# Residual kept in its own order, a step of eight in the gather's weights, and the router's matmuls in another order

## The chip, the cores and the metric

The kernel runs on one core of one Trainium2 chip. The metric is the device time of one execution in microseconds (us). The engines are TensorE (PE, with its weight loads listed as PEld), VectorE (DVE), ScalarE (ACT), GpSimd (POOL) and SyncE (SP), whose queue issues the large transfers.

## The reference, cut to what matters

The reference runs two transformer blocks over 256 tokens of width 1024. The first one ends with a mixture of 32 experts, chosen in two steps (one of 4 groups, then 2 of its 8 experts):

```python
x = x + gt1 * (merged @ w_out)
h2 = rmsnorm(x, norm2_g) * (1.0 + sc2) + sh2
group_logits = h2 @ rg_w + rg_b
exp_logits = (h2 @ re_w + re_b).reshape(-1, 4, 8)
g_sel = argmax(group_logits)
top_v, top_i = top_k(exp_logits of group g_sel, 2)
y = y + (silu(h2 @ w_gate[e]) * (h2 @ w_up[e]) * gate) @ w_down[e]   # for each chosen expert e
x = x + gt2 * y
```

## The kernel before, in words

Everything is fp32. Each large product is made of three matmuls of fp32r operands (high part and low part, lines 532 to 534), whose weights come from DRAM once. The kernel is one program in which each engine walks the same plan of weight pieces; semaphores join them. The five queues of orders are written out by hand, so an engine does its work in the order of the code.

The stretch around the change is this. The output projection `wo` ends in two column halves g of 512 (two token tiles t each). VectorE adds each result to the residual x (lines 2408 and 2411). ScalarE squares x for the norm (line 1635, `x_square`). TensorE transposes each 128 x 512 part of x (`x_turn`, line 795), ScalarE copies it to SBUF (`x_copy`, line 1627, into `rF`), and TensorE multiplies it with the scaled router weights, 36 columns (`router`, line 803). Logits of both token tiles are accumulated over g = 0 and g = 1. `warm(n)` (line 760) issues n matmuls whose results nobody reads; an fp32 matmul of this kind is two records in the trace, a transpose is one. ScalarE walks in the order square (1, 0), copy (1, 0), square (1, 1), copy (1, 1), square root of the sums.

The route is then a chain of some 15 small VectorE instructions (lines 2070 to 2111), after which TensorE forms ranks (`route`, lines 854 to 863), VectorE writes one-hot slot matrices `Sx` in three parts of 2, 3 and 3 sets of slots (`slots_of`, line 2031), and TensorE picks the tokens with them: `gather(g, banks)`, line 775, has x as the weights and `Sx` as the streaming operand. The first gather runs in `route()`, the other two in `experts()`, behind the first set's up and gate products. The gathers take x times the norm factor in two fp32r parts: the high part is written by ScalarE (`x_high`, line 1406), the low part by VectorE (`x_low`, line 2019), into `xs`. The expert products need 8 chunks k of the width; chunk k is made of columns k, k + 8, k + 16 and so on, since the expert weights lie so in DRAM. Before, `x_high` and `x_low` do this reordering while they read:

```python
inc(e.activation(by8(xs[0], i), x[:, i, :].rearrange("p (c k) -> p k c", k=8), ACT.Copy, ...
```

and a gather matmul takes its weights in one piece, `xs[part][:, i, 128 * k:128 * k + 128]`. Each gather has 32 matmuls: 8 chunks k times two parts times two token tiles. In the first one four banks are filled side by side through all four passes, which are ordered (part, tile) = (0, 0), (0, 1), (1, 0), (1, 1); VectorE does `x_low(0)`, `slots_of(0)`, `x_low(1)`, `slots_of(1)` in this order. VectorE (line 2043) and ScalarE (line 1418) evict the results in turn into `XG`.

Expert weights come through a ring of slots of 1 MB, 17 before the first use, 14 of them used again. The SyncE queue refills a slot when TensorE has done its last matmul on it (`("exu", q, s)`, given by `up` at line 888 and `down` at line 899).

Another place uses a step of 8 on the weights' side already: line 616, `acc[g][:, k:512:8]`, 64 columns, plain fp32.

Of the kernel before, what the change touches and what calls it, by code (L numbers as in the profile page):

```python
# [6 lines left out]
F32 = mybir.dt.float32  # L7
# [3 lines left out]
ALU = mybir.AluOpType  # L11
ACT = mybir.ActivationFunctionType
# [112 lines left out]
def rv(ap):  # L125
    return ap.bitcast(F32R)
# [6 lines left out]
def build(nc, a, out, scr):  # L133
    with ExitStack() as ctx:
# [3 lines left out]
        def mem(off, n):  # L138
            placed[0] += 1
            return nc.alloc_sbuf_tensor_at(f"m{placed[0]}", [128, n], F32, offset=base + 4 * off)[:, :]  # L140
# [27 lines left out]
        x = mem(22304, 2048).rearrange("p (t n) -> p t n", t=2)  # L168
# [12 lines left out]
        def K(c, n=128):  # L181
            return KC[:, c:c + n]
# [3 lines left out]
        def tiny(n):  # L186
            o = top[0]
            top[0] += n
            assert top[0] <= 512
            return small[:, o:o + n]  # L190
# [149 lines left out]
        def skey(p, what):  # L340

            return (what, p.j)
# [11 lines left out]
        ss1, ssr, ssf = tiny(2), tiny(2), [tiny(2) for _ in range(9)]  # L354
# [36 lines left out]
        xs = [rv(mem(o, 2048).rearrange("p (t n) -> p t n", t=2)) for o in (26912, 28960)]  # L391
# [34 lines left out]
        for n in range(4):  # L426
            o = 33312 if n == 2 else 29216
# [29 lines left out]

            return min(last_wo + 1 if p.j <= last_wo else len(plan), p.j + NH)

        def by8(z, i):  # L460

            return z[:, i, :].rearrange("p (k c) -> p k c", k=8)

        def heads(head):

            gens, h = [], 0
            while h < 8 or gens:
                if h < 8 and len(gens) < 5:
                    gens.append(head(h))
                    h += 1  # L470
                for g in list(gens):
                    if next(g, "end") == "end":
                        gens.remove(g)
                yield
# [32 lines left out]
        def tensor(e, w):  # L507
# [16 lines left out]
            def full(ins, *key):  # L524
                then_inc(ins, f"full{where_is[key]}", ("full", key))
# [17 lines left out]
            def parts(p, o, n):  # L543
                return rv(p.H)[:, o:o + n], rv(p.L)[:, o:o + n]
# [212 lines left out]
            def warm(n):  # L757

                for _ in range(n):
                    e.matmul(bank[where_is["wo", 0, 1]][:, 0:128], K(C_ID), K(C_ONE), start=True, stop=True)  # L760

            def gather(g, banks):

                q0, q1 = parts_of[g]
                n = 128 * (q1 - q0)
                per = 512 // n
                o = {}
                for ks in ([(0, 2, 4, 6), (1,), (3,), (5,), (7,)] if per > 1 else [(k,) for k in range(8)]):
                    for part, i in ((0, 0), (0, 1), (1, 0), (1, 1)):
                        w.wait_ge("xs", part, i)  # L770
                        w.wait_ge("Sx", g, i)
                        for k in ks:
                            if (part, i) == (0, 0) and k % per == 0:
                                o[k // per] = take(banks[k // per % len(banks)], "ga", g, k // per)
                            ins = e.matmul(o[k // per][:, k % per * n:k % per * n + n], xs[part][:, i, 128 * k:128 * k + 128],  # L775
                                           rv(Sx[:, i, 128 * q0:128 * q1]), start=(part, i) == (0, 0),
                                           stop=(part, i) == (1, 1))
                            if (part, i) == (1, 1) and k % per == per - 1:
                                full(ins, "ga", g, k // per)
# [8 lines left out]
            def x_turn(g, ts=(0, 1)):  # L788

                for t in ts:  # L790
                    w.wait_ge("x1", t, g)
                    b = take("s", "r", g, t)
                    for c in range(4):
                        o = 512 * g + 128 * c
                        ins = e.transpose(b[:, 128 * c:128 * c + 128], x[:, t, o:o + 128], K(C_ID))
                    full(ins, "r", g, t)

            def router(g, b, ts=(0, 1)):
                for t in ts:
                    w.wait_ge("taken", ("r", g, t))  # L800
                    w.wait_ge("rWg")
                    for c in range(4):
                        ins = e.matmul(b[t][:, 0:36], rF[g][:, c, 128 * t:128 * t + 128], rWg[:, 4 * g + c, :],
                                       start=g == 0 and c == 0, stop=g == 1 and c == 3)
                    if g:
                        full(ins, "lg", t)

            def w_out():
                o, lg = {}, {}

                def step(p, t):
                    for i in range(p.m):
                        k = p.k + i
                        w.wait_ge("mgL", k // 2)
                        if k == 0:
                            o[t] = take("m", "wo", p.g, t)
                        rows = slice(128 * t, 128 * t + 128)
                        ins = three(o[t][:, :], (mgT[0][:, k, rows], mgT[1][:, k, rows]), parts(p, 512 * i, 512),
                                    k == 0, k == 7)
                    return ins  # L820
                held = []
                for p in walk("wo"):
                    w.wait_ge(*skey(p, "L"))
                    if p.k < 4:
                        for t in range(2):
                            ins = step(p, t)
                        used(ins, p)
                        continue
                    held.append(p)
                    if p.k < 6:  # L830
                        if p.g:
                            x_turn(0)
                            lg = [take("s", "lg", t) for t in range(2)]
                        continue
                    for t in range(2):
                        for h in held:
                            ins = step(h, t)
                            if t:
                                used(ins, h, *([("wo", p.g, 1)] if h is p else []))
                        if t == 0:  # L840
                            full(ins, "wo", p.g, 0)
                    held.clear()
                    if p.g == 0:
                        continue
                    x_turn(1, (0,))
                    router(0, lg)
                    x_turn(1, (1,))
                    router(1, lg, (0,))
                    warm(3)
                    router(1, lg, (1,))  # L850
                    warm(10)

# [238 lines left out]
            for p in walk("ik"):  # L1091
                w.wait_ge(*skey(p, "L"))
                b = take("m", "ik")
                for k in range(8):
                    ins = three(b[:, 0:256], parts(p, 128 * k, 128), (hT[0][:, k, :], hT[1][:, k, :]), k == 0, k == 7)
                used(ins, p, ("ik",))
            for p in walk("iw"):
                w.wait_ge(*skey(p, "L"))
                for t in range(2):
                    b = take("m", "iw", t)  # L1100
                    rows = slice(128 * t, 128 * t + 128)
                    for k in range(8):
                        ins = three(b[:, 0:8], (hT[0][:, k, rows], hT[1][:, k, rows]), parts(p, 8 * k, 8), k == 0, k == 7)
# [33 lines left out]
            for q in range(2):  # L1137
                b = take("s", "ws", q)
                for g in range(4):
                    ins = e.transpose(b[:, 128 * g:128 * g + 128], wsr[:, 512 * q + 128 * g:512 * q + 128 * g + 128], K(C_ID))  # L1140
# [15 lines left out]
            for p in walk("kk"):  # L1156
                w.wait_ge(*skey(p, "L"))
                b = take("m", "kk2", p.g)
                for k in range(8):
                    w.wait_ge("kv", k // 2)  # L1160
                    ins = three(b[:, 0:256], parts(p, 128 * k, 128), (kvT[0][:, k, :], kvT[1][:, k, :]), k == 0, k == 7)
# [14 lines left out]
        def scalar(e, w):  # L1176
# [3 lines left out]
            def inc(ins, what, *keys):  # L1180
                then_inc(ins, "act_" + what, *keys)
# [220 lines left out]
            def x_high():  # L1402
                w.wait_ge(*skey(G["wo"][-1], "used"))
                for i in range(2):
                    w.wait_ge("rrec")
                    inc(e.activation(by8(xs[0], i), x[:, i, :].rearrange("p (c k) -> p k c", k=8), ACT.Copy,
                                     scale=ssr[:, i:i + 1]), "xs", ("xs", 0, i))

            def gather(g):
                q0, q1 = parts_of[g]  # L1410
# [133 lines left out]
            o = 0  # L1544
# [14 lines left out]
            for cp in range(4):  # L1559
                w.wait_ge("taken", ("h", cp))  # L1560
                o = slice(512 * cp, 512 * cp + 512)
# [141 lines left out]
        def vector(e, w):  # L1703
# [4 lines left out]
            def inc(ins, what, *keys):  # L1708
                then_inc(ins, "dve_" + what, *keys)
# [306 lines left out]

            def x_low(i):
                w.wait_ge("xs", 0, i)
                inc(e.scalar_tensor_tensor(out=by8(xs[1], i), in0=x[:, i, :].rearrange("p (c k) -> p k c", k=8),
                                           scalar=ssr[:, i:i + 1], in1=by8(xs[0], i).bitcast(F32), op0=ALU.mult,  # L2020
                                           op1=ALU.subtract), "xs", ("xs", 1, i))

            def slots_of(g):

# [316 lines left out]
            for cp in range(4):  # L2341
# [3 lines left out]
                o = slice(512 * cp, 512 * cp + 512)  # L2345
# [82 lines left out]
            for i in range(2):  # L2428
                for g in range(8):
# [4 lines left out]
                                                 op1=ALU.mult), "mix", i, g)  # L2434
# [392 lines left out]
```

## Time and profile before

| what | us |
|---|---|
| median of 3 runs (2296.68 to 2307.59) | 2299.89 |
| the profiled execution's own time | 2299.89 |
| its span, first to last instruction | 2297.8 |
| TensorE busy | 2003.5 |
| VectorE busy | 1092.4 |
| ScalarE busy | 857.8 |

Mean granted clock of TensorE: 0.954 of full speed. Durations come from the one profiled execution; its time is 2.1 us over its span. The page says which engines are busy; the chain that ended last says which of this work sets the end; the windows say what DMA and clock did meanwhile; the timeline gives starts and durations of single instructions.

### The profile page before, as it was taken

The numbers are of one execution on the slowest core, as the hardware profiler recorded it, in microseconds if no ns is written. First come the engines' busy times: TensorE is split into PE (matmuls) and PEld (weight loads), VectorE is DVE, ScalarE is ACT, GpSimd is POOL, SyncE is SP. The second block draws the span as 40 slices with busy tenths as digits, with TensorE's granted clock in tenths as the row PEclk, the third lists the DMA queues.
The fourth block names the chain that finished last, engine by engine and source line by source line (L and its number), as shares of the span: only waits on it lengthen the run. The fifth ranks groups of instructions, "written<-read, shape, count | busy, mean of one in ns | idle before, by whom it ended". The sixth has DMA issues, their size and how long they took to land.

```text
span 2297.8 us, 30304 instructions
## 1 busy us (share of the span) xinstructions
PE 2003.5 (87%) x12871; PEld 1627.8 (71%) x12871; DVE 1092.4 (48%) x1359; ACT 857.8 (37%) x1110; POOL 136.9 (6%) x112
## 2 busy tenths in 40 slices
PE   3998899999999767776759998799998999959998
PEld 2998788888997211111139997678998999858997
DVE  5545576557764111111135555654555555485554
ACT  2444335544443100000034444335445444554443
POOL 0013312000210000000000000200000000030000
PEclk9989899999999998889889999899999999999999
DMA  8542343557888999999965554544554555304551
GB/s 309 171 129 92 92 148 129 168 199 238 283 313 329 393 424 423 423 423 424 423 233 188 186 182 156 177 147 148 184 195 134 185 185 184 125 19 156 184 184 72
DMA packets 243935, 503.16 MB, mean 219 GB/s; under 512 B 9562, under 2 KB 163507, under 8 KB 218835
## 3 DMA queue, kind: packets, MB, share of 16 engines
q1 hardware_dynamic: 243136, 500.27, 60.4%
q8 instruction: 104, 1.70, 0.3%
q10 hardware_dynamic: 514, 0.73, 0.1%
q0 software_dynamic: 144, 0.17, 0.1%
q14 instruction: 37, 0.30, 0.0%
HBM read 500.07 MB, written 1.06 MB: 218 GB/s over the span
## 4 chain that ended last, share of the span: by engine, by line
PE 70%; DMA 17%; DVE 6%; ACT 3%; issue 2%; POOL 1%; SPq 0%; DVEq 0%; ACTq 0%; POOLq 0%
PE bank L532 20%; PE bank L534 20%; PE bank L533 20%; DMA m<-in_expert_w_up 7%; DMA m<-in_expert_w_gate 7%; PE bank L888 3%; PE bank L590 2%; DVE m L1735 1%; PE bank L643 1%; ACT m L1244 1%; DMA m<-in_ada_w 1%; DMA m<-in_expert_w_down 1%; DMA m<-in_w_in 1%; PE bank L775 1%; PE bank L899 0%
## 5 line engine op out<-in xcount | busy, mean ns | idle before, releaser
L532 PE MATMUL bank<-m,m 128*128 128x256 f32 (+2 forms) x3240 | 1026.3, 317 | 23.2 <-DVE m L1735 20.0
L533 PE MATMUL bank<-m,m 128*128 128x256 f32 (+2 forms) x3240 | 1012.4, 312 | 0.0
L534 PE MATMUL bank<-m,m 128*128 128x256 f32 (+2 forms) x3240 | 1012.2, 312 | 0.0
L1735 DVE TENSOR_TENSOR m<-m,m 128x1024 fp32r<-128x1024 f32 x508 | 629.2, 1242 | 490.1 <-ACT m L1201 488.8
L1201 ACT ACTIVATE m<-m 128x1024 fp32r<-128x1024 f32 x508 | 534.7, 1058 | 463.1 <-PE bank L534 432.5
L532 PEld LDWEIGHTS bank<-m,m 128*128 128x128 f32 x3240 | 617.9, 191 | 67.1 <-DVE m L1735 22.2
L533 PEld LDWEIGHTS bank<-m,m 128*128 128x128 f32 x3240 | 617.9, 191 | 38.4 <-issue 2.4
L534 PEld LDWEIGHTS bank<-m,m 128*128 128x128 f32 x3240 | 616.8, 190 | 37.1
L888 PE MATMUL bank<-m,m 128*32 128x512 f32 x1024 | 192.5, 690 | 72.8 <-DMA m<-in_expert_w_up 47.6
L888 PEld LDWEIGHTS bank<-m,m 128*32 128x32 f32 x1024 | 42.0, 123 | 213.3 <-DMA m<-in_expert_w_up 86.8
L899 PE MATMUL bank<-m,m 128*32 128x512 f32 x512 | 96.8, 677 | 44.0 <-DMA m<-in_expert_w_down 36.9
L899 PEld LDWEIGHTS bank<-m,m 128*32 128x32 f32 x512 | 21.1, 120 | 113.3 <-DMA m<-in_expert_w_down 70.7
L2165 DVE SCALAR_TENSOR_TENSOR m<-bank,m,m 128x512 f32<-128x512 f32 x8 | 6.0, 750 | 173.3 <-PE bank L888 173.3
L590 PE MATMUL bank<-m,m 128*128 128x128 f32 x256 | 43.2, 348 | 47.3 <-DVE m L1797 41.4
L2171 DVE TENSOR_TENSOR m<-bank,m 128x512 f32<-128x512 f32 x16 | 10.3, 686 | 150.9 <-PE bank L899 150.9
L590 PEld LDWEIGHTS bank<-m,m 128*128 128x128 f32 x256 | 42.1, 262 | 49.8 <-issue 49.8
L1491 ACT ACTIVATE m<-m 128x512 fp32r<-128x512 f32 x44 | 27.8, 632 | 107.7 <-DVE m L2244 107.7
L1749 DVE SCALAR_TENSOR_TENSOR m<-m,m,m 128x512 f32<-128x512 f32 x84 | 63.1, 751 | 8.3 <-DMA m<-in_ada_w 5.5
L1430 ACT ACTIVATE m<-m 128x512 fp32r<-128x512 f32 x16 | 9.3, 630 | 142.3 <-DVE m L2171 142.3
L1447 ACT ACTIVATE m<-bank 128x512 f32<-128x512 f32 x8 | 4.8, 597 | 147.3 <-PE bank L923 147.3
L1485 ACT ACTIVATE m<-bank 128x512 f32<-128x512 f32 x44 | 26.3, 598 | 71.1 <-PE bank L534 71.1
L2562 POOL TENSOR_TENSOR m<-m,m 128x2048 f32<-128x2048 f32 x1 | 6.6, 6601 | 774.0 <-DMA m<-in_a_ln_b 774.0
(312 smaller groups left out, 1286.1 us busy)
## 6 DMA issues: line engine op xcount, KB each, us to landing
m<-in_ffn_w_in SPq DMA_DIRECT2D x88, 1024.0 KB, 5.1
m<-in_w_in SPq DMA_DIRECT2D x66, 1024.0 KB, 5.1
m<-in_expert_w_gate SPq DMA_DIRECT2D x64, 1024.0 KB, 25.5
m<-in_expert_w_up SPq DMA_DIRECT2D x64, 1024.0 KB, 24.2
m<-in_expert_w_down SPq DMA_DIRECT2D x64, 1024.0 KB, 25.6
m<-in_ffn_w_out SPq DMA_DIRECT2D x44, 1024.0 KB, 4.9
m<-in_ada_w SPq DMA_DIRECT2D x24, 1024.0 KB, 5.5
m<-in_a_w_in SPq DMA_DIRECT2D x16, 1024.0 KB, 5.2
```

What stands on the lines that cost most here:

```text
L532: e.matmul(o, s[0], m[0], start=first, stop=False, skip_group_check=skip)
L533: e.matmul(o, s[0], m[1], start=False, stop=False, skip_group_check=skip)
L534: return e.matmul(o, s[1], m[0], start=False, stop=last, skip_group_check=skip)
L590: ins = e.matmul(o, v, D[:, 128 * (i % 2):128 * (i % 2) + 128], start=True, stop=True)
L643: ins = e.matmul(b[:, 128 * g:128 * g + 128], K_[:, c], Q_[:, c2], start=True, stop=True)
L888: ins = e.matmul(b[32 * j:32 * j + 32, :], XG[:, q, k, 32 * j:32 * j + 32], ld.raw[:, 512 * i:512 * i + 512], start=k == 0, stop=k == 7, s ...
L899: ins = e.matmul(b[n][32 * j:32 * j + 32, :], eT[q % 2][:, 128 * c + 32 * j:128 * c + 32 * j + 32], ld.raw[:, 1024 * i + 512 * n:1024 * i ...
L1201: inc(e.activation(rv(fit(q.H, q.view.shape)), q.view, ACT.Copy), "h", skey(q, "H"))
L1485: taken(e.activation(fb[4], b[:, :], ACT.Silu), p.name, p.g, also=[("fs", n, c)])
L1491: inc(e.activation(fb[2 * (c % 2)].rearrange("p c n -> p (c n)"), fb[5], ACT.Copy), "ffn", ("fH", n, c))
L1735: inc(e.tensor_tensor(rv(fit(q.L, q.view.shape)), q.view, fit(q.H, q.view.shape), ALU.subtract), "l", skey(q, "L"))
L1749: ins = e.scalar_tensor_tensor(out=acc[g], in0=p.view[:, k, :], scalar=cs[:, 4 * q + k:4 * q + k + 1], in1=acc[g], op0=ALU.mult, op1=ALU.add)
```

## The change

`x_high` and `x_low` write `xs` in the order of x, and the helper `by8` is gone. The gathers take chunk k as every eighth column of `xs`, with a step of 8 elements (32 bytes) from one weight column to the next. At the end of the output projection, `router(0)` stands ahead of the transposes of (1, 0); the second transposes follow `router(1)` of tile 0; and three groups of `warm` (4, 2 and 4 matmuls) take the place of one of 3. The last `warm(10)` stays.

```diff
--- before.py
+++ after.py
@@ -457,10 +457,6 @@
 
             return min(last_wo + 1 if p.j <= last_wo else len(plan), p.j + NH)
 
-        def by8(z, i):
-
-            return z[:, i, :].rearrange("p (k c) -> p k c", k=8)
-
         def heads(head):
 
             gens, h = [], 0
@@ -772,7 +768,7 @@
                         for k in ks:
                             if (part, i) == (0, 0) and k % per == 0:
                                 o[k // per] = take(banks[k // per % len(banks)], "ga", g, k // per)
-                            ins = e.matmul(o[k // per][:, k % per * n:k % per * n + n], xs[part][:, i, 128 * k:128 * k + 128],
+                            ins = e.matmul(o[k // per][:, k % per * n:k % per * n + n], xs[part][:, i, k:1024:8],
                                            rv(Sx[:, i, 128 * q0:128 * q1]), start=(part, i) == (0, 0),
                                            stop=(part, i) == (1, 1))
                             if (part, i) == (1, 1) and k % per == per - 1:
@@ -842,11 +838,13 @@
                     held.clear()
                     if p.g == 0:
                         continue
+                    router(0, lg)
                     x_turn(1, (0,))
-                    router(0, lg)
+                    warm(4)
+                    router(1, lg, (0,))
+                    warm(2)
                     x_turn(1, (1,))
-                    router(1, lg, (0,))
-                    warm(3)
+                    warm(4)
                     router(1, lg, (1,))
                     warm(10)
 
@@ -1403,8 +1401,7 @@
                 w.wait_ge(*skey(G["wo"][-1], "used"))
                 for i in range(2):
                     w.wait_ge("rrec")
-                    inc(e.activation(by8(xs[0], i), x[:, i, :].rearrange("p (c k) -> p k c", k=8), ACT.Copy,
-                                     scale=ssr[:, i:i + 1]), "xs", ("xs", 0, i))
+                    inc(e.activation(xs[0][:, i, :], x[:, i, :], ACT.Copy, scale=ssr[:, i:i + 1]), "xs", ("xs", 0, i))
 
             def gather(g):
                 q0, q1 = parts_of[g]
@@ -2016,9 +2013,8 @@
 
             def x_low(i):
                 w.wait_ge("xs", 0, i)
-                inc(e.scalar_tensor_tensor(out=by8(xs[1], i), in0=x[:, i, :].rearrange("p (c k) -> p k c", k=8),
-                                           scalar=ssr[:, i:i + 1], in1=by8(xs[0], i).bitcast(F32), op0=ALU.mult,
-                                           op1=ALU.subtract), "xs", ("xs", 1, i))
+                inc(e.scalar_tensor_tensor(out=xs[1][:, i, :], in0=x[:, i, :], scalar=ssr[:, i:i + 1],
+                                           in1=xs[0][:, i, :].bitcast(F32), op0=ALU.mult, op1=ALU.subtract), "xs", ("xs", 1, i))
 
             def slots_of(g):
```

## Rows read from the trace of the kernel before

**Rows 1.** The page, shares of the chain that ended last, by engine.
```profile
PE 70%; DMA 17%; DVE 6%; ACT 3%; issue 2%; POOL 1%; SPq 0%; DVEq 0%; ACTq 0%; POOLq 0%
```

**Rows 2.** The chain in order of time (start us, us, what).
```profile
713.55 2.06 DVE m L2019
...
715.66 2.65 PE bank L775 x20
...
737.61 11.31 PE bank L775 x64
...
765.59 21.18 DMA m<-in_expert_w_up
```

**Rows 3.** Windows: busy us (instructions) by engine, clock, DMA share, GB/s.
```profile
716.00:718.00 2.00, 2.00 (x19) 2.00 (x18) 1.70 (x6) 0.61 (x2) 0.00 (x0) 1.00 0.00 0
...
758.00:759.00 1.00, 1.00 (x16) 0.36 (x12) 0.00 (x0) 0.00 (x0) 0.00 (x0) 1.00 0.00 0
900.00:1000.00 100.00, 70.45 (x343) 16.16 (x337) 9.24 (x14) 4.13 (x7) 0.00 (x0) 0.86 1.01 423
```

**Rows 4.** Vector lines: duration ns min/median/max, first and last start, form.
```profile
L1201 ACT ACTIVATE m<-m x508: 250/1060/1166, 36.1 to 2276.6; 128x1024 fp32r<-128x1024 f32 x170
...
L1406 ACT ACTIVATE m<-m,m x2: 2138/2148/2157, 706.5 to 708.5; 128x1024 fp32r<-128x1024 f32 x2
...
L2222 DVE SCALAR_TENSOR_TENSOR m<-m,m,m x4: 1277/1282/1285, 1180.3 to 2293.3; 128x1024 f32<-128x1024 f32 x4
...
L2019 DVE SCALAR_TENSOR_TENSOR m<-m,m,m x2: 2067/2105/2143, 710.8 to 713.5; 128x1024 fp32r<-128x1024 f32 x2
```

**Rows 5.** Timeline, 703 to 740 us (start us, us, engine, line).
```profile
703.02 1.87 PE L803 MATMUL bank<-m,m 128*128 128x36 f32 x16
...
704.72 0.64 PE L795 MATMUL bank<-m,m 128*128 128x128 f32 x4
...
705.39 0.60 ACT L1627 ACTIVATE m<-bank 128x512 f32<-128x512 f32 x1 [0.44 <-PE bank L795]
...
706.01 0.91 PE L760 MATMUL bank<-m 128*128 128x128 f32 x6
...
706.47 4.20 ACT L1406 ACTIVATE m<-m,m 128x1024 fp32r<-128x1024 f32 x2 [0.29 <-DVE m L2072]
...
706.76 0.98 PE L803 MATMUL bank<-m,m 128*128 128x36 f32 x8
...
710.83 2.07 DVE L2019 SCALAR_TENSOR_TENSOR m<-m,m,m 128x1024 fp32r<-128x1024 f32 x1
...
711.94 0.91 PE L760 MATMUL bank<-m 128*128 128x128 f32 x6
712.80 0.75 DVE L2031 TENSOR_TENSOR m<-m,bank 128x256 fp32r<-128x256 f32 x2
...
713.36 1.67 PE L775 MATMUL bank<-m,m 128*128 128x256 f32 x12 [0.51 <-DVE m L2031]
...
718.24 10.51 PE L888 MATMUL bank<-m,m 128*32 128x512 f32 x96
...
739.24 0.68 ACT L1418 ACTIVATE m<-bank,m 128x384 f32<-128x384 f32 x1 [13.26 <-PE bank L775]
```

**Rows 6.** Weight loads: three lines' durations as in rows 4, a timeline row.
```profile
L1064 PEld LDWEIGHTS bank<-m,m x32: 137/137/137, 2035.6 to 2066.2; 128*64 128x64 f32 x32
...
L775 PEld LDWEIGHTS bank<-m,m x96: 186/188/192, 713.3 to 748.4; 128*128 128x128 f32 x96
...
L616 PEld LDWEIGHTS bank<-m,m x64: 195/218/220, 471.6 to 555.5; 128*64 128x64 f32 x64
...
471.65 2.00 PEld L616 LDWEIGHTS bank<-m,m 128*64 128x64 f32 x16
```

**Rows 7.** Windows, columns as in rows 3.
```profile
708.00:710.00 2.00, 2.00 (x19) 1.86 (x17) 1.79 (x12) 2.00 (x2) 0.00 (x0) 1.00 1.01 422
...
732.40:735.60 3.20, 3.20 (x17) 0.78 (x20) 0.38 (x2) 0.00 (x0) 0.00 (x0) 0.50 1.01 428
```

## The prediction

> **What bounds the kernel now.** I read the page's shares of the chain first, to see which parts of the program can set the end at all. TensorE holds 70% and DMAs 17% [rows 1]. The diff touches one stretch only: the end of the output projection, the router, and the gathering of tokens for the experts, about 702 to 749 us. So the question is whether this stretch is on the chain. The chain in order of time says yes: it goes through VectorE's `x_low(1)` at 713.55, then TensorE's gather matmuls at 715.66 and 737.61, and only at 765.59 does it pass to the DMAs of the expert weights [rows 2].
>
> Next I asked whether the DMA stream absorbs a delay of TensorE, since it fills the experts' time. The windows say no. The stream runs at 423 GB/s through the experts, but it stands at 0 GB/s at 716 to 718 us and again at 758 to 759 us [rows 3]. Both times every slot of the ring is full, and a slot comes free only when TensorE has used it: `up(0, 0)` comes right behind the first gather, `down(0, 4)` behind the second and third. After the second gap the share stays at 1.01, so the end of the experts is the end of that gap plus a fixed number of bytes. A delay of the gathers delays the first restart by the first gather's part and the second restart by the whole. It passes one for one to the end, and so does a gain. Nothing of 700 to 760 us is free on TensorE; VectorE and ScalarE matter only where TensorE waits for them.
>
> **Part 1: contiguous writing of the residual.** In the kernel before, `x_high` and `x_low` read x with a step of 8 elements. They take 2148 and 2105 ns apiece for 1024 elements; the contiguous neighbours of the same width, a ScalarE copy and a VectorE scalar_tensor_tensor, take 1060 and 1282 ns [rows 4]. So the two on ScalarE give up 2 x 1.09 = 2.2 us, and the two on VectorE 2 x 0.82 = 1.6 us. ScalarE's gain counts nothing: its pair started at 706.47 and had ended when VectorE began `x_low(0)` at 710.83 [rows 5], and after it starts at about 708.7 and ends at 710.9, under the route's small VectorE chain, which ends at 712.6 (part 2). Were that cover gone it would be worth up to 2.2 us. VectorE's 0.82 us of `x_low(0)` lies ahead of `slots_of(0)`, for which the first gather waits; that of `x_low(1)` ends the pause in the middle of that gather (below).
>
> **Part 2: the order on TensorE.** I count records. Between the last projection matmul and the end of the last `router(1)`, before has 16 of `router(0)`, 4 transposes, 4 transposes, 8, 6 of `warm(3)` and 8, which is 46. After has the same work with 4 + 2 + 4 warm matmuls in place of 3, which is 14 records more. A warm record takes (706.76 - 706.01)/6 = 0.125 us, a router record (704.72 - 703.02)/16 = 0.106 us [rows 5]. By that 14 x 0.125 = +1.75 us. Does TensorE wait besides? By the same rows `router(0)` starts four transposes before 703.02, at 702.6, and ends at 704.3, the transposes of (1, 0) end at about 704.9, and their copy on ScalarE (0.60 us [rows 5]) at about 705.5, under `warm(4)`, which lasts to 705.75. The transposes of (1, 1) end at 707.7, their copy at 708.3, under `warm(4)` again, to 708.54. So no wait is added, and the last `router` starts at 708.5 where it started at 706.76. VectorE's logits for t = 1 wait for it, and with them the whole route: +1.75 us. On ScalarE the square of (1, 1) now stands behind a later copy, and the square root behind both; it comes at about 708.3, the reciprocal at 708.5, still ahead of the logits at 709.5. Without warm matmuls' cost the move would be nearly neutral.
>
> Together: `x_low(0)` starts at 710.83 + 1.75 = 712.58. `slots_of(0)` started 1.97 us behind it and now does so 1.15 us behind, at 713.73 (the ranks stand ahead of `warm(3)` on TensorE and are there). TensorE started 0.56 us after that, at 713.36; by this it would at 714.29, but its own `warm(3)`, six records from 711.94 [rows 5], leaves it free 1.75 us later than it did, at 711.94 + 0.75 + 1.75 = 714.44. So the first gather starts there, **+1.08 us**. Its pause is gone: the fourth pass needed `x_low(1)`, for which it stood until 715.66 [rows 2]; now that ends at 713.73 + 0.66 + 1.28 = 715.7 and TensorE comes to it after 12 matmuls, not before 716.0.
>
> **Part 3: the gather's weights with a step of 8.** This decides. Each of the 96 gather matmuls loads 128 columns of `xs` as weights, contiguous before and 32 bytes apart after. The trace of before has no strided fp32r load of 128 columns, so I bound it. Contiguous loads take 137 ns for 64 columns and 188 for 128 [rows 6]: a fixed 86 ns and 0.80 ns a column, so that 128 columns hold the loader for some 102 ns. Line 616 has exactly the new step, `acc[g][:, k:512:8]`, with 64 columns: 195 ns at least and 218 at the median, against 137. Less 86 that is 109 to 132 ns for 64 columns, and 16 of them in a row span 2.00 us, so one each (2.00 - 0.22)/15 = 0.119 us [rows 6]. Doubled, these are 0.218 to 0.264 for 128 columns, with 0.238 between. The other engines pay alike for the same step: (2148 - 1060)/1024 = 1.06 ns more an element on ScalarE [rows 4], and the weights (119/64 - 0.80) = 1.06 ns more a column. I take 0.24 us, twice the measured spacing. The ends that I keep are 0.129 (no cost, below) and 0.350 us (86 + 2 x 132, no load overlapping the next one).
>
> The weights can be loaded while the matmul before runs, so a gather matmul takes the longer of load and stream. Before, the first gather's last 20 took (718.24 - 715.66)/20 = 0.129 us [rows 2, 5], and the 64 of the other two, 384 wide, 11.31 us or 0.177 us each [rows 2]. Then:
> - first gather: 32 x 0.24 = 7.68 us in place of 718.24 - 713.36 = 4.88 us, which is +2.80; with the late start **+3.88 us**
> - second and third: 64 x 0.24 = 15.36 in place of 11.31, **+4.05 us**. The evictions, 0.67 us a bank on alternating engines [rows 5], stay under 4 x 0.24 = 0.96, since a bank holds one k and takes four matmuls.
>
> Sum +7.9 us. The profiled execution took 2299.89 us (span 2297.8, the rest lies around it), which is also the median of the three, so the forecast is 2299.9 + 7.9 = **2307.8 us**, +0.34%. With 0.218 it is 1.08 + 2.10 + 2.64 = +5.8 (2305.7), with 0.264 it is 1.08 + 3.57 + 5.59 = +10.2 (2310.1): the forecast's own range, with a little of noise, is 2305 to 2311.
>
> **Rivals.** *The step costs the weight load nothing.* For it: nothing but that line 616 is plain fp32 in two records, and a load of 64 columns. Against it: 218 ns beside 137. Then the first gather is 32 x 0.129 = 4.1 us from 714.44, it ends at 718.55, and all is +0.3 us: 2300.2. 
>
> *The loads don't overlap at all.* One mechanism: each strided load holds the loader for its full 350 ns. Then 32 x 0.350 = 11.2 (+6.3, with the start +7.4) and 64 x 0.350 = 22.4 (+11.1), +18.5 us: 2318.4, slower by 0.8%. Against it: line 616 starts a load every 119 ns while each lasts 218. It decides (over 11.5 us) from 0.277 us a load, where 96 loads cost the missing 3.6 us more.
>
> *The clock falls.* The granted clock went to 0.50, the lower level of 1.2 GHz, at 732.4 to 735.6 us, behind `slot_gates`, whose matmuls stream four columns each [rows 7]. The strided loads thin TensorE's stream of columns as well. If the clock fell through the second and third gather, a matmul of 384 columns would take 384/1.2 = 0.32 us in place of 0.24: 64 x 0.08 = +5.1 more, 2312.9. Against: behind the router's 36-column matmuls the clock is 1.00 at 708 to 710 [rows 7], and behind the pause in the first gather it is 1.00 at 716 to 718 [rows 3].
>
> *Faster.* The step free and the route not late either, because the copies on ScalarE were what ended last. Then the first gather starts at about 712.9 and ends at 717.0, -1.3 us: 2298.6. The records before show no wait of the router for a copy, which speaks against it; and even that is not 0.5%.
>
> **How the numbers follow.** Chances: forecast 0.62, step free 0.15, loads apart 0.09, clock 0.11, faster route 0.03. The range is 2299 to 2314: it takes in the free step and the clock and leaves out most of the loads apart and of the faster route. About 0.5% (11.5 us) is what a measurement can tell from no change. Faster by more than that: 0.03, for noise alone, as no case gives it. Slower: loads apart and the clock case nearly whole, and the upper end of the forecast: 0.27. Same: 0.70.
>
> **What the profile after would show.** Weight loads of the gather line at about 350 ns instead of 188, and matmuls 0.24 us apart in all three gathers; 1.06 us for `x_high` and 1.28 us for `x_low`; the last `router` about 1.75 us later; no pause in the first gather; DMA gaps that end about 3.9 and 7.9 us later. Wrong would be loads of 190 ns (then 2300), spacings over 0.28 us, or a DMA stream that still restarts at 759 us, by which the delay would have been absorbed.

## The result: 0.5% slower, and the profile after

| | us |
|---|---|
| before, median of 9 | 2300.91 |
| changed, median of 9 | 2313.01 |
| ratio | 1.0051, 95% interval 1.0039 to 1.0062 |
| the profiled execution of the changed kernel | 2311.64, span 2309.6 |

The ratio stands for +11.7 us, with an interval of 9.0 to 14.3. A second set of runs of the same kernel (e8 below) gave 1.0043, 1.0027 to 1.0059, which is +9.9 us. The forecast was +7.9 us, 2307.8, with 2305 to 2311 for the forecast case alone; the measured 2313.0 lies outside that and inside the whole range of 2299 to 2314.

The gather line decided the forecast, so it comes first. These are its weight loads and its matmuls in the profile after: duration in ns (min/median/max), then first and last start.

```profile
L771 PEld LDWEIGHTS bank<-m,m x96: 312/338/343, 709.4 to 753.5; 128*128 128x128 f32 x96
L771 PE MATMUL bank<-m,m x96: 352/404/570, 709.4 to 753.7; 128*128 128x384 f32 x64, 128*128 128x256 f32 x32
```

A load takes 338 ns where it took 188 [rows 6]. The timeline after answers to [rows 5]:

```profile
703.51 1.04 PE L799 MATMUL bank<-m,m 128*128 128x36 f32 x8
...
703.90 2.19 ACT L1404 ACTIVATE m<-m,m 128x1024 fp32r<-128x1024 f32 x2 [0.30 <-DVE m L2068]
...
707.63 1.28 DVE L2016 SCALAR_TENSOR_TENSOR m<-m,m,m 128x1024 fp32r<-128x1024 f32 x1
...
708.75 0.91 PE L756 MATMUL bank<-m 128*128 128x128 f32 x6
708.83 0.75 DVE L2027 TENSOR_TENSOR m<-m,bank 128x256 fp32r<-128x256 f32 x2
...
709.42 7.97 PE L771 MATMUL bank<-m,m 128*128 128x256 f32 x32
...
717.32 10.51 PE L886 MATMUL bank<-m,m 128*32 128x512 f32 x96
```

The times of this stretch are nearly all earlier than before, although the kernel is slower: the parts ahead of the diff vary from one execution to the next. So the two can only be laid over each other from a common point. I take VectorE's last product of the output projection (line 2408, in the changed kernel 2404), which is the last start in these rows of before and of the changed kernel:

```profile
L2408 DVE TENSOR_TENSOR m<-bank,m x4: 684/692/692, 691.6 to 702.8; 128x512 f32<-128x512 f32 x4
```
```profile
L2404 DVE TENSOR_TENSOR m<-bank,m x4: 683/690/692, 686.8 to 697.9; 128x512 f32<-128x512 f32 x4
```

Counted from there, the points in the table repeat to 0.1 us between the two executions of before, of the changed kernel and of e6. The table has all kernels of this study, in us from the common point: the start of the first expert matmul (`up(0, 0)`), of the first of `down(0, 4)`, and the landing of the last expert weights, for which TensorE waits on the chain.

| kernel | common point (us from the start) | `up(0, 0)` | `down(0, 4)` | last weights |
|---|---|---|---|---|
| before | 702.8 | +15.4 | +51.9 | +461.5 |
| before again (e11) | 699.4 | +15.5 | +51.9 | +461.5 |
| changed | 697.9 | +19.4 | +61.9 | +472.7 |
| changed again (e8) | 699.4 | +19.4 | +61.9 | +472.6 |
| e1 order only | 700.3 | +17.2 | +55.3 | +464.9 |
| e2 step only | 700.9 | +17.7 | +56.9 | +468.3 |
| e3 neither | 699.6 | +13.8 | +48.6 | +458.2 |
| e4 steps 1 to 8 | 699.9 | +16.3 | +55.2 | +465.0 |
| e5 delay | 697.8 | +24.8 | +61.3 | +470.8 |
| e6 `down` first | 701.9 | +15.4 | +37.2 | +457.4 |
| e12 the same again | 699.1 | +15.5 | +37.3 | +457.3 |
| e7 `down` first, changed kernel | 699.9 | +19.4 | +41.2 | +463.9 |
| e9 as e6, no inner warm | 701.1 | +14.9 | +36.7 | +456.7 |
| e10 order without warm | 698.2 | +20.0 | +54.8 | +465.3 |

So the changed kernel has its last expert weights 11.2 us later. The chain after (start us, us, what), to be read beside [rows 2], says where most of them come from:

```profile
709.66 7.72 PE bank L771 x32
717.39 10.44 PE bank L886 x96
727.82 4.39 PE bank L868 x32
732.21 6.14 PE bank L886 x32
738.36 15.74 PE bank L771 x64
```

The first gather has no pause and 0.241 us a matmul; the other two take 15.74 us where they took 11.31. In between, `slot_gates` and `up(0, 3)` take 10.53 us. The same two rows of before are

```profile
728.74 3.71 PE bank L870 x32
732.45 5.16 PE bank L888 x32
```

that is 8.87 us, with the same instructions. The windows of the changed kernel tell why (busy us by engine, clock, DMA share, GB/s; to be read beside [rows 3, 7]):

```profile
710.00:712.00 2.00, 2.00 (x10) 2.00 (x9) 1.79 (x4) 0.00 (x0) 0.00 (x0) 0.52 0.03 12
712.00:714.00 2.00, 2.00 (x10) 2.00 (x10) 0.00 (x0) 0.00 (x0) 0.00 (x0) 0.63 0.00 0
714.00:716.00 2.00, 2.00 (x10) 2.00 (x10) 0.99 (x2) 0.49 (x2) 0.00 (x0) 1.00 0.00 0
732.00:736.00 4.00, 4.00 (x21) 1.11 (x25) 0.38 (x2) 0.00 (x0) 0.00 (x0) 0.50 1.01 426
...
762.00:764.00 2.00, 2.00 (x24) 0.77 (x20) 0.00 (x0) 0.00 (x0) 0.00 (x0) 1.00 0.03 8
764.00:766.00 2.00, 2.00 (x24) 0.79 (x20) 0.00 (x0) 0.00 (x0) 0.00 (x0) 1.00 0.73 168
```

The lower clock lasts longer between the gathers than it did. It is also there in the first gather, where ten matmuls pass in 2 us at 0.52, at 0.63 and at 1.00 alike. That gather goes at the pace of its weight loads, and the clock costs it nothing: it took 7.72 us here, and 7.70 in e7 below, where the same gather ran wholly at 1.00. The second stop of the DMA stream ends after 764 us, which is +66 from the common point; before it ended after 759, which is +56 [rows 3].

### The profile page after: what moved, and what is told of

It reads as the page before. It is cut to its first block, busy times and chain, and to the rows that moved or that the text cites. A ratio compares the mean times of both kernels' runs of the same rounds, so it can differ in the third digit from the quotient of the medians.

```text
span 2309.6 us, 30332 instructions
## 1 busy us (share of the span) xinstructions
PE 2021.6 (88%) x12885; PEld 1638.4 (71%) x12885; DVE 1089.7 (47%) x1359; ACT 855.4 (37%) x1110; POOL 136.6 (6%) x112
## 4 chain that ended last, share of the span: by engine, by line
PE 71%; DMA 16%; DVE 6%; ACT 3%; issue 2%; POOL 1%; SPq 0%; ACTq 0%; DVEq 0%; POOLq 0%
PE bank L528 20%; PE bank L530 20%; PE bank L529 20%; DMA m<-in_expert_w_up 7%; DMA m<-in_expert_w_gate 6%; PE bank L886 3%; PE bank L586 2%; DVE m L1732 1%; PE bank L771 1%; PE bank L639 1%; ACT m L1242 1%; DMA m<-in_expert_w_down 1%; DMA m<-in_w_in 1%; PE bank L897 1%; DMA m<-in_ada_w 0%
## 5 line engine op out<-in xcount | busy, mean ns | idle before, releaser
L530 PEld LDWEIGHTS bank<-m,m 128*128 128x128 f32 x3240 | 615.9, 190 | 37.2
L886 PE MATMUL bank<-m,m 128*32 128x512 f32 x1024 | 198.1, 715 | 73.0 <-DMA m<-in_expert_w_up 46.6
L897 PE MATMUL bank<-m,m 128*32 128x512 f32 x512 | 99.9, 697 | 39.4 <-DMA m<-in_expert_w_down 32.2
L586 PEld LDWEIGHTS bank<-m,m 128*128 128x128 f32 x256 | 41.7, 260 | 48.6 <-issue 48.6
```

Of the source, the lines that this page charges most:

```text
L530: return e.matmul(o, s[1], m[0], start=False, stop=last, skip_group_check=skip)
L586: ins = e.matmul(o, v, D[:, 128 * (i % 2):128 * (i % 2) + 128], start=True, stop=True)
L886: ins = e.matmul(b[32 * j:32 * j + 32, :], XG[:, q, k, 32 * j:32 * j + 32], ld.raw[:, 512 * i:512 * i + 512], start=k == 0, stop=k == 7, s ...
L897: ins = e.matmul(b[n][32 * j:32 * j + 32, :], eT[q % 2][:, 128 * c + 32 * j:128 * c + 32 * j + 32], ld.raw[:, 1024 * i + 512 * n:1024 * i ...
```

## The experiments

**The parts of the diff, one at a time.** The first one keeps the old gather and the old writing and takes the new order:

```diff
-                    x_turn(1, (0,))
                     router(0, lg)
-                    x_turn(1, (1,))
+                    x_turn(1, (0,))
+                    warm(4)
                     router(1, lg, (0,))
-                    warm(3)
+                    warm(2)
+                    x_turn(1, (1,))
+                    warm(4)
                     router(1, lg, (1,))
```

> The kernel before with TensorE's new order at the end of the output projection and nothing else: x is still read with the step, the gather's weights are contiguous. Measured from the end of the output projection. Theory (14 more warm records push the whole route): last router 1.7 us later, first gather starts 1.7 us later, its pause stays, and all ends +1.7 us, 2302.6 where before has 2300.9. Rival (the order is what costs, by the clock or by a wait for a copy on ScalarE): +5 us or more, and a stall ahead of a router in the trace.

Measured: 1.0025, 1.0013 to 1.0036, +5.8 us. In the trace the route came 1.7 us later, `up(0, 0)` 1.8 us, and there was no stall. Another 1.7 us came behind it, again between the gathers:

```profile
714.86 2.66 PE bank L775 x20
...
727.96 4.67 PE bank L872 x32
732.63 5.86 PE bank L890 x32
738.49 11.34 PE bank L775 x64
```

4.67 + 5.86 = 10.53 us as in the changed kernel, and the last weights come 3.4 us later. The theory of the 14 records holds for its part, 1.7 us. As a forecast of the whole time, +1.7 us, it failed: the interval, 3.0 to 8.3 us, leaves it out, and the number is the rival's (+5 or more), though the stall that the rival asked for is not there. What the trace does explain is 3.4 us, near the lower end of the interval; anything above that is unexplained.

The second one is the changed kernel with the old order at that place.

> The changed kernel with TensorE's old order at the end of the output projection: contiguous xs, weights with the step of 8. Theory: first gather starts 0.7 us earlier than before, since x_low(0) is shorter, takes 7.7 us, ends 2.1 us later than before; the other two take 15.7 us in place of 11.3 (+4.4); with 1.7 us of lower clock behind slot_gates as in the changed kernel that is +8.2 us at the end. Weight loads 338 ns. Rival (the order costs most): no more than +4 us. Rival (the clock fell because of the new order): the 1.7 us of slower matmuls between the gathers are gone.

Measured: 1.0029, 1.0019 to 1.0038, +6.7 us. Its chain:

```profile
710.98 7.71 PE bank L771 x32
...
729.13 3.67 PE bank L866 x32
732.80 3.57 PE bank L884 x32
736.37 15.75 PE bank L771 x64
```

`up(0, 0)` is at +17.7, 2.3 later (2.1 expected). Here no time is lost between the gathers: 3.67 + 3.57 = 7.24 us, less than before's 8.87. The lower clock came later, in `down(0, 4)`:

```profile
756.00:758.00 2.00, 0.88 (x8) 0.74 (x12) 0.00 (x0) 0.69 (x2) 0.00 (x0) 1.00 0.18 74
758.00:760.00 2.00, 2.00 (x12) 0.54 (x8) 0.00 (x0) 0.00 (x0) 0.00 (x0) 0.52 0.00 0
760.00:762.00 2.00, 2.00 (x16) 0.70 (x12) 0.00 (x0) 0.00 (x0) 0.00 (x0) 0.63 0.00 0
```

and the last weights are 6.8 us later. This is what the clock rival foretold for the place between the gathers; but the fall moved rather than went, so it doesn't show that the order causes it. The kernel e7 below answers this.

The third one takes the step away too:

```diff
-  xs[part][:, i, k:1024:8]
+  xs[part][:, i, 128 * k:128 * k + 128]
```

> As the run before it, with contiguous weights: chunk k is columns 128 k to 128 k + 127 instead of every eighth column, so the experts get their inputs in a wrong order, while each instruction but the weight loads is the same. Theory (only the step costs): weight loads back to 188 ns, first gather about 4.1 us without a pause and ended 1.4 us earlier than before, the other two at 11.3 us, total -1.4 us, 2299.5. Rival (the contiguous writing itself or the lost pause costs): not faster than before, +1 us or more.

By this the experts get the columns of x in another order; but for the step of the loads, every instruction is that of e2. Measured: 0.9985, 0.9971 to 0.9998, -3.5 us (0.5 to 6.7 us faster). Loads are at 188 ns again, `up(0, 0)` is 1.6 us earlier than before, and as no low clock fell between the gathers, `down(0, 4)` is 3.3 earlier. Half of that, 1.6 us, is the clock. Against e2 the only difference is the step of the weights: 1.0029 against 0.9985 is 10 us, in the last weights 468.3 - 458.2 = 10.1 us, of which 17.7 - 13.8 = 3.9 in the first gather and 15.75 - 11.31 = 4.4 in the others; 1.7 of the remaining 1.8 us are e2's lower clock in `down(0, 4)` (8.77 us for 7.07). So contiguous writing is worth 1.6 us, and the step that pays for it costs 8.3 us.

**The load by its step.** The fourth gives every chunk k a step of k + 1 at a line of its own, as `z[:, 0:1017:8]` for k = 7, where `z` is `xs[part][:, i, :]`. Its chunks are then not those that the experts need; only the loads are of interest.

> As e2, but chunk k takes its weights with a step of k + 1 elements from column 0, each step at a line of its own, so its output is not the reference's. One look, for the weight load by step. Theory (16-byte lines: what fits several to a line is free): steps 1 and 2 at 188 ns, 3 in between, 4 and above slower; step 4 (16 bytes) about 240 ns and step 8 (32 bytes) 338. Rival (any step costs the same): 338 ns for all from 2 up. Rival (only powers of two collide): steps 5 and 7 well below step 8 and near step 4.

The lines of steps 2 to 8:

```profile
L776 PEld LDWEIGHTS bank<-m,m x12: 193/194/217, 712.7 to 743.4; 128*128 128x128 f32 x12
...
L778 PEld LDWEIGHTS bank<-m,m x12: 252/252/255, 709.8 to 744.1; 128*128 128x128 f32 x12
...
L780 PEld LDWEIGHTS bank<-m,m x12: 308/329/333, 713.2 to 745.0; 128*128 128x128 f32 x12
...
L782 PEld LDWEIGHTS bank<-m,m x12: 308/321/325, 710.0 to 745.9; 128*128 128x128 f32 x12
...
L784 PEld LDWEIGHTS bank<-m,m x12: 318/326/328, 714.1 to 746.8; 128*128 128x128 f32 x12
...
L786 PEld LDWEIGHTS bank<-m,m x12: 327/332/337, 710.2 to 747.8; 128*128 128x128 f32 x12
...
L788 PEld LDWEIGHTS bank<-m,m x12: 335/340/342, 715.0 to 748.7; 128*128 128x128 f32 x12
```

Step 2 is nearly free (194 ns), step 3 costs 252, and from 4 on it is 321 to 340, whether a power of two or not. The expectation of 240 ns for step 4 was wrong, and both rivals fell. The Trainium skill ("Advanced Engine Details and Errata", section SBUF Cachelines) has 16-byte lines and asks for at least two hits on each for full speed; four fp32 columns fill such a line. The trace agrees: steps 1 and 2 have at least two columns in a line, step 3 has one or two, from step 4 on each column has its own. A stream of 384-column matmuls feels it only from step 4: in this chain four of them took 0.71 us at step 3 and 0.93 us at step 4, against 11.31/16 = 0.71 with contiguous weights.

**Does a delay pass one for one?** The fifth is the kernel before with `warm(49)` ahead of the first gather.

> The kernel before with 49 more warm matmuls (98 records, 11.4 us) right ahead of the first gather. The gather then ends 10.0 us later than before, the whole delay that the touched stretch of the changed kernel shows in its trace. Theory (a delay here passes one for one to the end, through the stop of the DMA stream): total +10.0 us, 2311. Rival (something behind the stretch grows too, as the traces' further +2 us in the experts suggest): +12 us or more. Rival (absorbed by the DMA queue): under +6 us.

Measured: 1.0038, 1.0024 to 1.0052, +8.7 us. The trace has the delay at +9.4 us in `up(0, 0)` (a little less than the 10.0 reckoned), +9.4 in `down(0, 4)`, +9.3 in the last weights. The interval of the whole time, 5.5 to 12.0 us, excludes neither rival at its ends; the trace, 9.4 us in and 9.3 out, decides: a delay passes one for one, with no part of the diff in it.

**A way out of it.** The sixth moves the first set's `down(0, 4)` ahead of the second and third gather, in all three engines' orders; on TensorE:

```diff
                     up(q, 3, b)
-                    if q == 0:
-                        gather(1, (4, 5, 6, 7))
-                        gather(2, (4, 5, 6, 7))
-                        slots_turned()
...
                     down(q, 4, b)
+                    if q == 0:
+                        gather(1, (4, 5, 1, 3))
+                        gather(2, (4, 5, 1, 3))
+                        slots_turned()
                     down(q, 5, b)
```

> The kernel before with down(0, 4) of the first set ahead of the second and third gather, which take banks 4, 5, 1 and 3; VectorE and ScalarE follow. The slots of down(0, 4) then come free while the DMA stream still has work. Theory (the second stop of the stream, 755 to 759 us, is on the path): the stop is gone and all ends 4.2 us earlier, 2296.7, and only the first stop is left. Rival (the stream is not what ends last there): within 1 us of before.

Measured: 0.9987, 0.9975 to 0.9999, -3.0 us. Where the DMA stream stood before, it now runs:

```profile
754.00:756.00 2.00, 1.20 (x10) 0.65 (x8) 0.07 (x1) 1.66 (x5) 0.00 (x0) 1.00 1.05 438
756.00:758.00 2.00, 1.80 (x12) 0.95 (x16) 0.00 (x0) 1.50 (x5) 0.00 (x0) 1.00 0.98 410
758.00:760.00 2.00, 2.00 (x24) 0.65 (x20) 0.00 (x0) 0.04 (x1) 0.00 (x0) 1.00 1.02 430
```

The last weights come 4.1 us earlier. In this execution the 26 matmuls behind them took 6.58 us where before's took 3.63, which hides most of it in the one trace. It was run again:

> e6 once more. Its trace took away the second stop of the DMA stream and had the last expert weights 4.1 us earlier, but its last matmuls ran at half clock. Theory: -4 us against before; in the interval of e6 (-0.2 to -5.8 us). Rival: no change.

Measured: 0.9991, 0.9982 to 1.0001, -2.1 us, with the last weights 4.2 us earlier. The second interval, -4.1 to +0.2 us, still holds no change at its end. The two intervals overlap from -0.2 to -4.1 us, so the trace's 4.1 us is at their edge: the stop is closed in both traces, and the whole time gained by it is 2 to 3 us as measured.

The same move in the changed kernel:

> The same move in the changed kernel. Theory: the 4.4 us that the strided weights cost in the second and third gather, and the second stop, are hidden under the DMA stream; what is left is the first gather's +3.9 us and about 0.7 us of clock ahead of it against the 4.2 us gained, so about before, 2301, and 12 us under the changed kernel less what varies. Rival (the cost stays on the path): 4 us under the changed kernel at most, 2309.

Measured: 1.0027, 1.0014 to 1.0041, +6.2 us. The last weights are 2.4 us later than before and 8.8 us earlier than in the changed kernel. A part of the second stop is left there, since `down(0, 5)` now waits for two strided gathers:

```profile
764.00:766.00 2.00, 2.00 (x20) 0.60 (x24) 0.00 (x0) 0.42 (x2) 0.00 (x0) 1.00 1.03 434
766.00:768.00 2.00, 2.00 (x24) 0.65 (x20) 0.36 (x1) 0.00 (x0) 0.00 (x0) 1.00 0.41 168
768.00:770.00 2.00, 2.00 (x24) 0.56 (x20) 1.77 (x4) 1.17 (x2) 0.00 (x0) 1.00 0.73 160
```

So the move took the wait away only for the most part. The whole time gained 3.7 us against the changed kernel by the ratios (e8 was measured beside it), which is the rival's number (4 us at most) and not the theory's 12.

Not all of the 8.8 us in the trace is the move's. Here is this kernel's stretch between `up(0, 2)` and the end of `up(0, 3)`:

```profile
729.81 3.67 PE bank L868 x32
733.47 5.31 PE bank L886 x32
```

That is 8.98 us where the changed kernel took 10.53, and up to there TensorE has the same instructions in the same order in both. So 1.6 us of the 8.8 are another course of the clock, and 7.2 are left for the move. The difference from 7.2 to 3.7 us is not explained; the intervals of the two ratios are each about 3 us to either side.

This also bears on the rival that the new order makes the clock fall longer. The stretch took 10.53 to 10.55 us in the changed kernel, e8 and e1, but 8.98 in e7 and 7.24 in e10, all with the new order; with the old order it took 7.24 in e2 and e3 and 8.87 to 8.98 in the other seven traces. The new order alone doesn't bring the longer fall, since e7 and the changed kernel differ by nothing ahead of it; that it makes it likelier is not excluded.

The ninth adds to e6 a shorter way to the last router: `warm(3)` goes behind it, which makes `warm(10)` a `warm(13)`.

> e6 with the three warm matmuls between the last two routers moved behind them. Theory: the last router starts 0.66 us earlier (706.1 where it was 706.76) and with it the route and the first restart of the DMA stream; total -4.1 - 0.7 = -4.8 us against before, 2296. Rival (ScalarE's copy or the square root ends last then): no more than e6 gave. Rival (clock): the clock falls earlier, +2 us.

Measured: 0.9971, 0.9959 to 0.9983, -6.7 us (3.9 to 9.4 us faster), and so faster than both kernels (median 2294.0 beside 2299.3 for before, measured with it). `up(0, 0)` comes 0.5 us earlier, the last weights 4.8 us earlier, as expected. Beside e12, measured with it, the time is 4.6 us shorter by the ratios, where the traces show 0.6; the shorter route alone does not account for the rest, and no run says what does.

**What the warm matmuls are for.** The tenth has the new order without the warm matmuls between the routers.

> e1 without the warm matmuls of 4, 2 and 4 between the routers, and warm(20) at the end. One look. Theory (the records are what e1's +1.7 us are made of, and without them TensorE waits twice for ScalarE's copy): last router starts 1.0 us later than before, counted from the end of the output projection, with two stalls of about 0.7 us ahead of the routers. Rival (the new order alone costs nothing, all was warm records): last router no later than before.

One execution, 2302.74 us. Its timeline at the routers, and windows:

```profile
700.36 0.60 ACT L1626 ACTIVATE m<-bank 128x512 f32<-128x512 f32 x1 [2.78 <-PE bank L795]
...
701.01 1.08 PE L803 MATMUL bank<-m,m 128*128 128x36 f32 x8 [0.69 <-ACT m L1626]
...
703.25 1.82 PE L803 MATMUL bank<-m,m 128*128 128x36 f32 x8 [0.69 <-ACT m L1626]
```
```profile
702.00:704.00 2.00, 1.31 (x9) 1.07 (x9) 0.42 (x2) 1.11 (x3) 0.00 (x0) 0.85 1.01 422
704.00:706.00 2.00, 2.00 (x11) 2.00 (x11) 0.79 (x5) 2.00 (x2) 0.00 (x0) 0.50 1.02 430
```

The last router starts 703.25 - 698.2 = 5.05 us after the common point, before 706.76 - 702.8 = 3.96: +1.1 us, with two stalls of 0.69 us, as expected. What was not expected: the clock fell behind the two stalls, in this one execution. The last router took 1.82 us instead of 0.98, and my `warm(20)` at the end kept TensorE's queue until 712 us, so that the ranks were late. Its +20.0 for `up(0, 0)` is therefore this kernel's own and no price of the order.

**The two kernels once more**, to see what belongs to them and what to the execution.

> The changed kernel once more. Theory: +11 to +12 us; the stretch from the end of the output projection to the slot transposes again +10.0 us, and the parts ahead of it and behind it, which differed by -4.8 us and +6.6 us between the two profiled executions, come out otherwise, as they hold the same instructions. Rival (those parts are changed by the diff): the same -4.8 and +6.6 us again.

> The kernel before once more, one look. Theory: counted from the end of the output projection the first matmul of the experts is again at 15.4 us and that of down(0) at 51.9 us, give or take 1.7 us of lower clock; the part ahead of it is not again 4.8 us longer than in the changed kernel, nor the part behind the experts shorter, but as the granted clock falls. Rival (the two kernels differ there too): same 702.8 and same tail as in the first profile.

The points of the stretch repeated in both (table above). The common point moved by 3.4 us in the kernel before and by 1.5 in the changed one. Behind the experts the same matmuls take longer where the mean granted clock is lower. These are windows over the same work, from the norm of the first block to a later product (line 1140), in before, changed and e1 (TensorE's busy time, clock, DMA share, GB/s):

```profile
1180.30:1395.50 215.20, 199.77 (x1384) 0.95 0.51 169
```
```profile
1187.30:1404.90 217.60, 202.23 (x1385) 0.94 0.51 167
```
```profile
1181.30:1394.50 213.20, 197.75 (x1384) 0.96 0.52 171
```

In e8 this stretch took 217.7 us, in before again 216.7. So in the first pair of profiles the 4.9 us less ahead of the common point and the 5.5 us more behind the last expert weights are mostly of the execution. They cancelled by chance, so that the pair's difference, 11.8 us, came near the measured one. The second pair needs no such luck: e8 and before again have the same common point, 699.4 us, and of their spans' difference, 2312.6 - 2300.9 = 11.7 us, 11.1 are there at the last expert weights.

## Why the prediction came out as it did, step by step

The time lay in the range, 1 us under its upper end, and at the very bound of 0.5% between same and slower. The forecast of +7.9 us was too small by 2 to 4 us. It was partly luck that the range held: its upper part was there for a clock that falls in the second and third gather, and the clock cost its 1.7 us elsewhere.

- *The stretch is on the path and passes one for one.* Right, shown by e5 (9.4 us in, 9.3 us at the last weights) and e6 (the second stop taken away, the last weights 4.1 us earlier). But that nothing of 700 to 760 us is free on TensorE held only for the order as it stood: e6 puts the second and third gather where the stream does not wait for them.
- *Part 1.* 1140 ns for `x_high`, 1280 for `x_low`, against 1060 and 1282 forecast. Worth 1.6 us with the pause gone (e3), as reckoned from `x_low` alone, though that sum stood nowhere as a gain of its own.
- *Part 2, +1.75 us.* Right: +1.7 us (e1), no wait on ScalarE. The first gather started at 709.42 - 697.9 = 11.52 us from the common point, before 713.36 - 702.8 = 10.56: +0.96 for the forecast +1.08.
- *Part 3, 0.24 us a load.* Right: 0.241 us in the first gather, 15.74/64 = 0.246 in the others. The first took 3.0 us more than before (2.8 forecast), the others 4.4 (4.05). Doubling line 616's spacing for twice the columns was a good estimate; its duration, 218 ns for 64 columns, less the fixed part and doubled would have given 350 against 338.
- *The sum.* Mis-sized: its terms measured 1.0 + 3.0 + 4.4 = 8.4 us, and 2.8 us of the 11.2 at the last weights are in no term. 1.7 us is the clock between the gathers, 10.53 us for 8.87. The prediction held the clock for a rival and looked for its price in the second and third gather, where it never fell; it did not ask whether the fall behind `slot_gates`, which it quoted, would last as long again. The other 1.2 us come behind `down(0, 4)`, in both profiles of the changed kernel and in neither of before. The DMA windows there show only a few microseconds at 328 to 377 GB/s, which is not enough. The step in the weights is not needed for it: e10, with contiguous weights, has 465.3 - 54.8 = 410.5 us from `down(0, 4)` to the last weights, against 409.6 in before and 410.8 in changed. The cause stays open.
- *Rivals.* The free step and the loads apart are refuted by 338 ns and 0.24 us. The Trainium skill's rule that the prediction quotes for the free step ("TensorE: Matmul & The Clock Gate", section LDWEIGHTS) counts columns and doesn't mention a step; "whatever their step" was the prediction's own reading, and 188 against 338 ns for the same 128 columns shows it wrong. The faster route is refuted by e1. The clock came in part, in another place and for 1.7 us instead of 5.1. The same instructions ahead of it gave the longer fall in the changed kernel and the shorter in e7, so those 1.7 us belong to an execution as much as to the diff.

## What to carry to other kernels

A reordering has to be paid by one reader or writer, and it should be the one that does it once: two reads with a step of 8 cost the vector engines 1.6 us of the path, the same step in 96 weight loads cost 8.3. Steps of 1 or 2 fp32 elements in a weight load were free or nearly so, and from 4 on the load was what matmuls of 256 and 384 columns waited for. When a stream of transfers has stops, ask which release ends each stop; moving one consumer ahead of unrelated work closed a stop of 4 us, for 2 to 3 us of the whole time; together with a shorter route -6.7 us were measured, of which the trace explains 4.8. And before a few microseconds are put down to an edit, see whether a kernel with the same instructions up to that point shows them too.

## What of the hardware was not expected

- A strided fp32 weight load of 128 columns has its full price at a step of 4 already (329 ns; 340 at 8; 321 at 5), 252 at 3, 194 at 2.
- A gather bound by such loads runs at the same pace at a granted clock of 0.52, 0.63 and 1.00: ten matmuls in each 2 us, and 7.72 us for the whole against 7.70 with the clock at 1.00 throughout (e7).
- The clock fell behind two stalls of 0.69 us among 36-column matmuls in the one execution of e10, and stayed at 1.00 there with warm matmuls in their place (e1, changed). One execution does not show that the stalls were the cause.
- With the same instructions ahead of them, the 64 matmuls between the gathers took 10.53 us in one execution and 8.98 in another (changed, e7).
